# First modulation computed as rows instead of columns, and a negated row maximum in window attention

## The reference

```python
def ada_modulation(c, w, b):
    mod = (jax.nn.silu(c) @ w + b)[:, None, :]
    return jnp.split(mod, 3, axis=-1)          # shift, scale, gate
...
shift, scale, gate = ada_modulation(c, ada_w[layer, 0], ada_b[layer, 0])
h = x * (1.0 + scale) + shift
z = h @ ab_w_in[i]                             # layer 0: one projection for both mixers
...
# layer 1: attention over a window of 128 tokens, 16 query heads of 64, 4 key heads
s = jnp.einsum('nqhgd,nkhd->nhgqk', qs, ks).astype(f32) * scale
s = jnp.where(valid[:, None, None], s, -jnp.inf)
m = jnp.maximum(s.max(-1, keepdims=True), sink_g)
p = jnp.exp(s - m)
denom = p.sum(-1, keepdims=True) + jnp.exp(sink_g - m)
return jnp.einsum('nhgqk,nkhd->nqhgd', (p / denom).astype(vs.dtype), vs)
```

## Time and profile before

| | us |
|---|---|
| median of 3 runs | 3812.29 |
| the three runs | 3812.64, 3800.78, 3812.29 |
| profiled execution | 3810.38 |
| its span, first to last instruction | 3808.4 |
| TensorE busy | 3275.3 (86%) |
| VectorE busy | 2060.8 (54%) |
| ScalarE busy | 1235.2 (32%) |
| GpSimd busy | 312.6 (8%) |
| mean granted TensorE clock | 0.91 of full |

### The profile page before, as it was taken

The page is one execution under the profiler, slowest core; times in us unless marked ns, Lnnn a source line. Parts: engine busy times, 40 slices in busy tenths (PEclk is TensorE's granted clock), DMA queues, the critical chain, the costliest instruction groups (busy, mean ns, idle before and its releaser), DMA issues. The chain is left out here.

```text
span 3808.4 us, 44180 instructions
## 1 busy us (share of the span) xinstructions
PE 3275.3 (86%) x15440; PEld 2158.7 (57%) x15440; DVE 2060.8 (54%) x4152; ACT 1235.2 (32%) x2952; POOL 312.6 (8%) x393
## 2 busy tenths in 40 slices
PE   8999999689999977995986999599788879499980
PEld 7555555378888876983543444244466645344430
DVE  1886685399999946884762001354355523500108
ACT  1112222244444425653641222122344423122212
POOL 0000100100000011110000010110000000001011
PEclk6999999689999978997987999799899989699995
DMA  7444233511111012226416999732221152299986
GB/s 245 144 151 151 63 106 116 186 34 37 36 37 37 27 47 77 92 84 200 164 67 227 362 365 364 271 133 89 86 77 56 51 176 94 106 338 361 365 291 220
DMA packets 367022, 583.85 MB, mean 153 GB/s; under 512 B 56692, under 2 KB 262004, under 8 KB 366600
## 3 DMA queue, kind: packets, MB, share of 16 engines
q1 hardware_dynamic: 296312, 356.20, 28.5%
q0 software_dynamic: 31312, 110.26, 8.2%
q10 hardware_dynamic: 39232, 115.22, 7.8%
HBM read 456.93 MB, written 124.68 MB: 153 GB/s over the span
## 5 line engine op out<-in xcount | busy, mean ns | idle before, releaser
L359 PE MATMUL inp__bank<-inp__hT,inp__w 128*128 128x512 f32 (+1 forms) x1536 | 560.2, 523 | 0.5 <-issue 0.5
L2586 PE MATMUL moe__bank<-moe__wgu,moe__xT 128*128 128x512 f32 x1024 | 456.6, 599 | 14.0 <-DMA moe__wgu<-in_moe_w_up_dram 12.6
L359 PEld LDWEIGHTS inp__bank<-inp__hT,inp__w 128*128 128x128 f32 x1536 | 289.5, 191 | 254.4 <-issue 240.4
L2586 PEld LDWEIGHTS moe__bank<-moe__wgu,moe__xT 128*128 128x128 f32 x1024 | 191.3, 192 | 234.9 <-issue 222.1
L2096 PE MATMUL close__bank<-close__w_out,close__catT 128*128 128x512 f32 x640 | 285.5, 600 | 21.0 <-DMA close__w_out<-in_at_w_out_dram 10.4
L2704 DVE TENSOR_TENSOR moe__hid<-moe__sg,moe__bank 128x256 f32<-128x256 f32 x64 | 27.0, 421 | 486.4 <-ACT moe__sg L2647 486.4
L2603 PE MATMUL moe__bank<-moe__wdn,moe__hidT 128*128 128x512 f32 x512 | 230.5, 593 | 2.9 <-ACT moe__hidT L2651 2.9
L2986 PE MATMUL cq__bank<-cq__w,cq__hT 128*128 128x512 f32 x480 | 211.7, 598 | 12.4 <-DMA cq__w<-in_at_w_in_dram 12.4
L2096 PEld LDWEIGHTS close__bank<-close__w_out,close__catT 128*128 128x128 f32 x640 | 120.7, 192 | 167.0 <-issue 140.2
L514 DVE SCALAR_TENSOR_TENSOR inp__acc_m<-inp__wv,inp__c_silu,inp__acc_m 128x1024 f32<-128x1024 f32 x140 | 179.7, 1284 | 4.5
L425 ACT ACTIVATE inp__z<-inp__bank 128x512 f32<-128x512 f32 (+1 forms) x96 | 50.5, 526 | 404.3 <-PE inp__bank L359 404.3
(11 more groups left out here) (459 smaller groups left out, 5973.7 us busy)
## 6 DMA issues: line engine op xcount, KB each, us to landing
moe__wdn<-in_moe_w_down_dram ACTq DMA_DIRECT2D x64, 1024.0 KB, 8.4
moe__wgu<-in_moe_w_gate_dram SPq DMA_DIRECT2D x64, 1024.0 KB, 7.2
moe__wgu<-in_moe_w_up_dram SPq DMA_DIRECT2D x64, 1024.0 KB, 14.6
inp__wv<-in_ada_w_dram SPq DMA_DIRECT2D x10, 4096.0 KB, 15.7
scratch_y_rows<-moe__y ACTq DMA_DIRECT2D x64, 512.0 KB, 8.8
scratch_zt<-inp__tb SPq DMA_DIRECT2D x32, 640.0 KB, 5.0
inp__w<-in_ab_w_in_dram POOLq DMA_DIRECT2D x31, 512.0 KB, 4.7
rwkv__rk<-scratch_zt SPq DMA_DIRECT2D x20, 512.0 KB, 3.9
```

The lines of the kernel that those rows point to most:

```text
L359: mm = pe.matmul(zbank[j][g][:, 0:n], w[:, j, k, :], hT[:, k, t0:t0 + n], start=k == 0, stop=k == KC - 1)
L2586: mm = pe.matmul(bank[2 + j][:], xT[:, j, k, :], wgu[:, j, k].rearrange("p a n -> p (a n)"), start=k == 0, stop=k == KC - 1)
```

## The change

The first edit is in the input projection. The roles of the operands are exchanged: the two columns of silu(c) are the weights and 512 columns of `wv` move, so that a piece takes 8 matmuls (`piece`) and its result is two rows of 512 in bank 6 or 7. VectorE adds the bias, also laid out as two rows, into `row0` (which lies in `work`; the bias row lies in `acc_m`). After the third group of transposes, `columns` turns the rows into 16 pairs of columns in bank 7, and VectorE copies them to `scol`. Pieces 2 and 3 wait until the row of the piece two before has been read. The loads of c move from SP's queue to ScalarE's, where the bias row takes the place of the bias column. Units 0 and 1 wait for the pieces as before, under another semaphore.

The second edit is in window attention. The score pass multiplies the masked score by -1 and takes the minimum with the negated sink; the result is the negated maximum itself, and the negating instruction of each head goes. exp gets scale -1. The sink is negated once ahead of the loop.

```diff
@@ input_projection, SP @@
                     if u < 2:
-                        sp.wait_ge(col_mm, 2 * u + 2)
+                        sp.wait_ge(piece_mm, 2 * u + 2)
...
-                for q, src in enumerate((a["c_prompt"], a["c_sample"])):
-                    sp.dma_start(c_col[:, :, q], src.rearrange("a (k p) -> p (a k)", p=P),
-                                 allow_slow_non_contiguous=True).then_inc(c_l, 16)
@@ input_projection, TensorE @@
-                def columns(n):
+                def piece(n):
                     pe.wait_ge(piece_l[n], 16)
-                    for b in range(4 * n, 4 * n + 4):
-                        for k in range(KC):
-                            mm = pe.matmul(bank[7][:, 2 * b:2 * b + 2], wv[:, n // 2, k, (b % 8) * P:(b % 8 + 1) * P], c_silu[:, k, :],
-                                           start=k == 0, stop=k == KC - 1)
+                    if n > 1:
+                        pe.wait_ge(row0_r, n - 1)
+                    for k in range(KC):
+                        mm = pe.matmul(bank[XB + n % 2][0:2, :], c_silu[:, k, :], wv[:, n // 2, k, (n % 2) * 512:(n % 2 + 1) * 512],
+                                       start=k == 0, stop=k == KC - 1)
+                    mm.then_inc(piece_mm, 1)
+
+                def columns():
+                    pe.wait_ge(row0_r, 4)
+                    for b in range(2 * KC):
+                        mm = pe.transpose(bank[7][:, 2 * b:2 * b + 2], row0[:, b * P:(b + 1) * P], ident[0:2, 0:2])
                     mm.then_inc(col_mm, 1)
@@ input_projection, ScalarE's queue @@
-                act.dma_start(bcol[:], a["ada_b"][0, 0, 0:2 * D].rearrange("(k p) -> p k", p=P),
-                              allow_slow_non_contiguous=True).then_inc(bcol_l, 16)
+                for q, src in enumerate((a["c_prompt"], a["c_sample"])):
+                    act.dma_start(c_col[:, :, q], src.rearrange("a (k p) -> p (a k)", p=P),
+                                  allow_slow_non_contiguous=True).then_inc(c_l, 16)
+                act.dma_start(brow, a["ada_b"][0, 0:1, 0:2 * D].broadcast_to([2, 2 * D])).then_inc(brow_l, 16)
@@ input_projection, VectorE @@
-                dve.wait_ge(bcol_l, 16)
-                mlink(dve.tensor_scalar(bcol[:, KC:], bcol[:, KC:], 1.0, None, ALU.add))
-                dve.wait_ge(col_mm, 4)
-                dve.tensor_tensor(scol[:], bank[7][:, 0:4 * KC].rearrange("p (b q) -> p b q", q=2),
-                                  bcol[:].unsqueeze(2).broadcast_to([P, 2 * KC, 2]), ALU.add).then_inc(scol_r, 1)
+                dve.wait_ge(brow_l, 16)
+                mlink(dve.tensor_scalar(brow[:, D:], brow[:, D:], 1.0, None, ALU.add))
+                for n in range(4):
+                    dve.wait_ge(piece_mm, n + 1)
+                    dve.tensor_tensor(row0[:, n * 512:(n + 1) * 512], bank[XB + n % 2][0:2, :], brow[:, n * 512:(n + 1) * 512],
+                                      ALU.add).then_inc(row0_r, 1)
+                dve.wait_ge(col_mm, 1)
+                dve.tensor_copy(scol[:].rearrange("p b q -> p (b q)"), bank[7][:, 0:4 * KC]).then_inc(scol_r, 1)
@@ window_attention, ScalarE @@
-                                act.wait_ge(n_r, i * AT_H + (n + 1))
-                                act.activation(s[:, n % 4], s[:, n % 4], ACT.Exp, bias=neg[:, n:n + 1],
+                                act.wait_ge(m_r, i * AT_H + (n + 4))
+                                act.activation(s[:, n % 4], s[:, n % 4], ACT.Exp, bias=neg[:, n:n + 1], scale=-1.0,
                                                accum_out=total[:, n:n + 1]).then_inc(e_r, 1)
@@ window_attention, VectorE @@
+                dve.tensor_scalar(sink_neg[:], sink[:], -1.0, None, ALU.mult).then_inc(negated, 1)
+                dve.wait_ge(negated, 1)
...
-                                dve.tensor_tensor_reduce(s[:, n % 4], bank[n % 3][:, 0:W3], band[:, j], 1.0, sink[:, n:n + 1],
-                                                         ALU.add, ALU.max, mx[:, n:n + 1]).then_inc(m_r, 1)
-                                dve.wait_ge(m_r, i * AT_H + (n + 4))
-                                dve.tensor_scalar(neg[:, n:n + 1], mx[:, n:n + 1], -1.0, None, ALU.mult).then_inc(n_r, 1)
+                                dve.tensor_tensor_reduce(s[:, n % 4], bank[n % 3][:, 0:W3], band[:, j], -1.0, sink_neg[:, n:n + 1],
+                                                         ALU.add, ALU.min, neg[:, n:n + 1]).then_inc(m_r, 1)
```

More of the change, by code:

```diff
@@ L201, in input_projection @@
         x = ph.sb("x", [P, XR, D])
-        bcol = ph.sb("bcol", [P, 2 * KC])
         scol = ph.sb("scol", [P, 2 * KC, 2])
@@ L206, in input_projection @@
         work = ph.sb("work", [P, 2 * D])
+        row0, brow = work[0:2, :], acc_m[0:2].rearrange("p q n -> p (q n)")
         part_sum = ph.sb("part_sum", [P, 2, 64])
@@ L225, in input_projection @@
         folded = bank[7][0:64, 0:32]
-        xt, raw, ht, prep, vec, vec_m, ident_l, fold_l, taps_l, c_l, bcol_l, bias_l, exp_done, silu_done, col_mm, scol_r = (
+        xt, raw, ht, prep, vec, vec_m, ident_l, fold_l, taps_l, c_l, brow_l, bias_l, exp_done, silu_done, piece_mm, row0_r, col_mm, scol_r = (
             ph.sem(n) for n in ("x_turned", "x_raw", "hT_ready", "prep", "vec", "vec_mod", "ident_loaded", "fold_loaded", "taps_loaded",
-                                "c_loaded", "bias_col_loaded", "bias_loaded", "exp_done", "silu_done", "columns_mm", "columns_ready"))
+                                "c_loaded", "bias_row_loaded", "bias_loaded", "exp_done", "silu_done", "piece_mm", "row0_ready", "columns_mm", "columns_ready"))
         x_l = [ph.sem(f"x_loaded{g}") for g in range(3)]
@@ L387, in _ @@
                 pe.wait_ge(silu_done, 1)
-                columns(0)
-                columns(1)
+                piece(0)
+                piece(1)
                 turn_rows(1)
-                columns(2)
-                columns(3)
+                piece(2)
+                piece(3)
                 turn_rows(2)
+                columns()
                 pe.wait_ge(fold_l, 16)
@@ L3175, in window_attention @@
         pT = ph.sb("pT", [P, 2, 3, P])
-        mx = ph.sb("mx", [P, AT_H])
+        sink_neg = ph.sb("sink_neg", [P, AT_H])
         neg = ph.sb("neg", [P, AT_H])
@@ L3181, in window_attention @@
         bank = ph.banks(8)
-        cst, in_free, s_mm, m_r, n_r, e_r, t_mm, o_mm, es_in, es_r, o_r, done, vec, init, step = (ph.sem(n) for n in (
-            "cst", "inputs_free", "scores_mm", "max_ready", "neg_ready", "exp_ready", "probs_turned", "out_mm",
+        cst, in_free, s_mm, m_r, negated, e_r, t_mm, o_mm, es_in, es_r, o_r, done, vec, init, step = (ph.sem(n) for n in (
+            "cst", "inputs_free", "scores_mm", "neg_max_ready", "sink_negated", "exp_ready", "probs_turned", "out_mm",
             "sink_diff", "sink_exp", "out_ready", "turn_done", "vec", "total_zeroed", "step"))
@@ L3311, in _ @@
                                 dve.tensor_copy(pT[:, 0].rearrange("p c t -> p (c t)"), bank[3][:, 0:W3]).then_inc(t_ev[0], 1)
-                        dve.wait_ge(n_r, i * AT_H + AT_H)
+                        dve.wait_ge(m_r, i * AT_H + (AT_H + 3))
                         dve.tensor_tensor(es[:], sink[:], neg[:], ALU.add).then_inc(es_in, 1)
```

## The result

| | before | after |
|---|---|---|
| median of 4 runs each, us | 3809.76 | 3762.46 |
| lowest and highest run, us | 3800.78, 3812.64 | 3748.17, 3769.88 |
| profiled execution and its span, us | 3810.38, 3808.4 | 3768.12, 3766.2 |
| mean granted clock | 0.910 | 0.917 |

The totals of the page after answer to the earlier trace rows: 176 TensorE instructions fewer, 155 fewer on VectorE.

The account below looks back on a forecast made before the run. TensorE was taken to bound the kernel, busy 3275.3 of 3808.4 us. 3810.4 - 25 (opening) - 12.4 (attention) = 3773.0, given as 3774 because the runs' median stood 1.9 higher; range 3764 to 3801.

Parts of the forecast that it names:

- Stream with two weight columns: Input stage: 256 records of 49.5 us replaced by 64 of 0.438 us, 28.0 us in all at full clock.
- Rival A: Input stage: the two-weight-column stream does not hold the clock; projection 1.9 us later, total 3802; chance 0.22.
- The rule weighed: Opening: by the skill's rule transposes don't bring full clock, pieces 0 and 2 cost 2 x 2.3 us more; trace preferred.
- Start and transfers: Opening: two issues leave SP's queue ahead of x, so x, pieces and TensorE's start move 1.1 us.
- Clock at the projection: Projection's start: full clock after a dense stream, saving 2.3 us lost before; one possible drop costs about 2.2.
- the term of 25: Opening's gain: projection 22.9 us sooner plus 2.3 us of clock is 25.2, kept as 25.
- Cover of VectorE: After the opening: VectorE may start its first chunk 4 us late, relatively, but has 23% idle; cost 0.
- rival B: Opening's gain half given back as taps and units come later and VectorE's backlog reaches TensorE; 3785.5 us; chance 0.08.
- Attention's turn: Attention: dropping the multiply shortens the two-head turn of 3.74 us by 0.19, 60 times, 11.4 us.
- C: Attention gains nothing because the turn closes over TensorE rather than over exp; 3785.4 us; chance 0.05.
- D: Attention: score pass takes longer with min and a scale; at 1.30 us a pass, 3826 us total; chance 0.03.
- the term for the tiles' starts: Attention: TensorE's wait for a tile's first exp, nine times, half counted, shortens by 0.19 each: 1.0 us.

Follow-up runs that it names:

- c_on_act: Kernel before with only c's loads moved from SP's to the head of ScalarE's queue, bias column kept; one run, 3815.03 us.
- after_again: The changed kernel once more, unchanged, for a second trace and a firmer time; median 3765.38 us, ratio 0.9885.
- before_again: The kernel before once more, unchanged, for a second trace; median 3813.37 us, ratio 1.0001.
- input_only: Kernel before with only the first edit (rows instead of columns in the opening), attention as before; median 3785.55 us, ratio 0.9929.
- attn_only: Kernel before with only the second edit (negation folded in attention), opening as before; median 3781.91 us, ratio 0.9917.
- copy_late: Changed kernel with a one-column VectorE instruction put back behind the score pass for heads 3 to 15 of each tile; median 3780.72 us.
- c_on_sp: Changed kernel with c's two loads back on SP's queue, ahead of the identity and x; one run, 3770.18 us.

## Why the prediction came out as it did

- **Stream with two weight columns.** Right: 64 records at 0.43 us (0.438 forecast), full clock from 16.5 to the projection. Rival A fell. What the term of 49.5 - 28.0 rests on is the clock alone, since at full clock both forms take about 28 us; rival A was the real alternative.
- **The rule weighed.** Pieces 0 and 2 began at full clock (1.00 in the us from 16, behind 6.5 us of transposes alone), so the 4.6 us of the rule did not come.
- **Start and transfers.** The start moved 2.0 us, not 1.1: x was issued 1.3 us sooner (1.17 instead of 2.46) and landed sooner after its issue. In `c_on_act`, with the bias column kept but issued behind x, the start moved as far (9.78), so the 2048 small packets need not go for it. The wait for piece 3, which I had under piece 2, took 0.94. Turns of the rows: 1.15 us instead of 2.1. Projection forecast at 55.0, measured at 52.9, 25.0 earlier.
- **Clock at the projection.** Wrong in the profiled execution: the clock fell at 53.5, and of the 2.3 us 0.6 came (ScalarE reads the end of the first chunk at 97.68 before and at 72.06 after, 25.6 sooner; the start is 25.0 sooner). In `after_again` the clock stayed full there. The text had named this possible drop. The earlier start and the missing clock cancel in the term of 25, which is luck in that term.
- **Cover of VectorE.** Right: z was ready at 72.4, mu and taps used at 72.7. The stage ends 25.6 us sooner, so rival B fell.
- **Attention's turn.** Right: 3.55 forecast, 3.56 measured, the pass unchanged at 617 ns. C and D fell. The sixty waits gave 19.1 - 6.9 = 12.2 us, against 11.4.
- **The failed step: the term for the tiles' starts,** "5 x 0.19 = 1.0". Measured, attention gained 10.9 us more than forecast. Of it 8.3 are the clock, a term that the sum had at nothing: I had read the wait at a tile's start by its length, not by the clock of the 4 us behind it, although the 21.0 us in nine waits stood in the earlier trace rows. The other 2 to 3 are the instruction itself: the first three heads gave 3.0 us in ten tiles instead of 1.0 for the starts, and the thirteen others 13.0 instead of 11.4. My upper bound of 16 for attention is about the gain at equal clock, 15 to 16, so it was a bound without the clock; and 5 us for the spread of runs, beside it, was short for a kernel whose four runs lie 21.7 apart.

What stays open. First, what decides the clock at a tile's start. At odd tiles 1.94 us of idle time lost it fifteen times of fifteen in before, `before_again` and `c_on_act`, and two of five in `input_only`; 1.75 to 1.77 lost it in none of twenty-five (after, `after_again`, `attn_only`, `copy_late`, `c_on_sp`); 1.95 and 2.39 in one of ten. At even tiles a wait of 2.6 to 2.9 us lost it 15 times of 16 with the code of before and 15 of 24 in the versions without the instruction or with half of it. Where in time the idle falls seems to matter, since `input_only` moves the same code by 25 us, but a move of 3 to 5 us (`before_again`, `c_on_act`) changed nothing; the turns between the waits are shorter in after too. I did not test either alone. Second, why the single edits' medians (28 and 32 us) add to 60 and the whole change to 47. Of the 13 us some 5 are attention's: 6.3 in `input_only` and 21.8 in `attn_only` are 28.1, and both together gave 23.3, as it would be if both won back the same lost clock. For the rest, the RWKV and DeltaNet stages vary with the same code: from the first record on `rwkv__KP` to the first on `delta__kqT`, and on to the first with `close__w_out`, the fourteen profiled executions took 694.7 to 707.9 and 331.8 to 338.4 us. That this noise is the cause is not shown.

## What to carry to other kernels

When a few columns multiply a large matrix, try both operands as the weights and compare the granted clock, not the count of matmuls. Here the streamed form took 28.0 us instead of 49.5 because it kept the clock; at full clock both take about as long. When an instruction leaves a closed turn, price the turns by the chain, and then read the granted clock in the few us behind each place where TensorE waits: a shorter wait can give back the clock, which was a third of attention's gain here. Move a load to another queue only after looking at what is queued behind it there.

## What the runs showed of the hardware

- A weight load of two columns took 0.09 us, one of 128 columns 0.19 at full clock; the records of 512 moving columns followed each other every 0.43 to 0.44 us in either case.
- Two moving columns on 128 weight columns came every 0.108 us at full clock and 0.21 at half.
- Gapless records of two moving columns lost the clock (0.50 at 22 us); two weight columns and 512 moving held it from 16.5 us to the projection's start at 52.9 through gaps of up to 0.94 us (in `c_on_sp` 1.27).
- Float32 transposes alone brought the full clock: TensorE had run nothing else from 9.95 us on when it was full at 16 us.
- Added matmuls in idle time made a stage shorter: 334.1 to 325.7 us in before, at a turn that stayed 3.74. The whole kernel's time did not clearly change.
- A small load's issue took 8.93 us behind the two loads of c and the bias column in one queue, 1.81 behind the bias column alone, and 0.37 behind c and the bias as a row.
- A row maximum turned into a minimum of the negative, with a scale of -1 in the same pass: 617 ns for 128x384 in both forms.
